# Two decoder blocks on one core: products of zeros ahead of the first unit, another order of the first loads, two query units over six blocks, another start of the banks' turn

## The reference, cut to what matters

```
def first_block(x, ...):                      # shortened
    h = rmsnorm(x, norm_mix_g)
    q, k, v, ... = split_cols(h @ w_in)       # 36 column units of 256
    x = x + merge(moba_attention(q, k, v), hgrn2(...)) @ w_out
    x = x + cross(rmsnorm(x, norm_x_g) @ wq_x, rmsnorm(mem, norm_mem_g) @ wkv_x) @ wo_x
    x = x + ffn(rmsnorm(x, norm_ffn_g))
def second_block(x, ...):
    for layer in range(2):
        x = x + 0.5 * swiglu(rmsnorm_2(x, ffn1_norm[layer]), ...)
        x = x + (nsa_mixer, diff_mixer)[layer](rmsnorm_2(x, mix_norm[layer]), ...)
        x = x + 0.5 * swiglu(rmsnorm_2(x, ffn2_norm[layer]), ...)
```

## Time and profile before

| | |
|---|---|
| median of 3 runs | 1664.88 us |
| lowest and highest | 1663.13, 1666.32 us |
| the profiled execution | 1664.09 us |
| its span, first to last instruction | 1662.3 us |
| mean granted clock of TensorE | 0.996 |
| instructions | 27264 |
| HBM | 281 MB read, 170 GB/s over the span |

### The profile page before, as it was taken

One profiled execution on the slowest core, in us unless ns is written; L12 is line 12 of the kernel. 1 busy time (PEld: TensorE's weight loads), 2 busy tenths in 40 slices (PEclk: granted clock), 3 DMA queues, 4 the chain that ended last, 5 costly groups with the idle time before them and its releaser, 6 DMA issues.

```text
span 1662.3 us, 27264 instructions
## 1 busy us (share of the span) xinstructions
PE 1626.0 (98%) x11542; PEld 1467.7 (88%) x11542; DVE 1222.1 (74%) x1481; ACT 929.5 (56%) x1249; POOL 153.4 (9%) x63
## 2 busy tenths in 40 slices
PE   7999999999999999999999899999999999999999
PEld 7999989999988888888987688888888898788888
DVE  6888868674588768986578868866887667678864
ACT  6966778455544455444387854444544457764442
POOL 0000000000022101220000002210222000002210
PEclk9999999999999999999999899999999999999999
DMA  7454434444355455545542235545554564345544
GB/s 258 180 199 153 153 129 151 178 172 159 129 204 199 140 192 212 208 163 173 199 178 103 103 120 195 192 153 202 209 197 160 177 223 146 109 147 185 192 157 130
DMA packets 44617, 283.80 MB, mean 171 GB/s; under 512 B 4944, under 2 KB 6608, under 8 KB 17744
## 3 DMA queue, kind: packets, MB, share of 16 engines
q1 hardware_dynamic: 44352, 281.99, 47.9%
q10 hardware_dynamic: 144, 0.08, 0.0%
HBM read 281.00 MB, written 1.05 MB: 170 GB/s over the span
## 4 chain that ended last, share of the span: by engine, by line
PE 83%; DVE 8%; ACT 7%; issue 2%; DMA 0%; DVEq 0%; ACTq 0%
PE bank L511 82%; ACT WH L1198 3%; DVE WL L1787 2%; DVE STAT L1945 1%; ACT SB L1323 1%; DVE HT L1843 0%; PE bank L676 0%; ACT XR L1205 0%; ACT XM L1205 0%; DVE XM L1795 0%; DVE SB L1942 0%; ACT FB L1222 0%; DVE FB L1813 0%; DMA PAR<-in_par 0%; DVE FA L2241 0%
## 5 line engine op out<-in xcount | busy, mean ns | idle before, releaser
L1787 DVE TENSOR_TENSOR WL<-RAW,WH 128x2048 fp32r<-128x2048 f32 (+1 forms) x282 | 590.0, 2095 | 165.3 <-ACT WH L1198 161.0
L1198 ACT ACTIVATE WH<-RAW 128x2048 fp32r<-128x2048 f32 (+1 forms) x282 | 494.1, 1755 | 360.6 <-PE bank L511 354.8
L511 PE MATMUL bank<-XR,WH 128*128 128x256 f32 (+1 forms) x2608 | 647.6, 327 | 12.2 <-DVE WL L1987 11.0
L511 PE MATMUL bank<-XR,WL 128*128 128x256 f32 x1832 | 515.6, 281 | 0.0
L511 PEld LDWEIGHTS bank<-XR,WH 128*128 128x128 f32 x2608 | 437.3, 189 | 58.4 <-DVE WL L1987 11.0
L511 PEld LDWEIGHTS bank<-XR,WL 128*128 128x128 f32 x1832 | 346.7, 189 | 0.1
L511 PE MATMUL bank<-XF,WH 128*128 128x512 f32 x880 | 305.3, 392 | 0.0
L511 PE MATMUL bank<-XM,WH 128*128 128x512 f32 (+1 forms) x960 | 290.9, 363 | 2.4 <-DVE XM L1828 1.3
L511 PE MATMUL bank<-XF,WL 128*128 128x256 f32 x880 | 246.0, 280 | 0.0
L511 PE MATMUL bank<-XM,WL 128*128 128x256 f32 x832 | 232.6, 280 | 0.0
L511 PEld LDWEIGHTS bank<-XM,WH 128*128 128x128 f32 x960 | 171.3, 188 | 32.9 <-DVE XM L1795 1.9
(11 more groups left out here) (285 smaller groups left out, 1719.6 us busy)
## 6 DMA issues: line engine op xcount, KB each, us to landing
RAW<-in_f1i SPq DMA_DIRECT2D x44, 1024.0 KB, 4.8
RAW<-in_f2i SPq DMA_DIRECT2D x44, 1024.0 KB, 4.8
RAW<-in_w_in SPq DMA_DIRECT2D x35, 1024.0 KB, 4.8
RAW<-in_w_ffn_in SPq DMA_DIRECT2D x22, 1024.0 KB, 4.8
RAW<-in_f1o SPq DMA_DIRECT2D x32, 704.0 KB, 4.2
RAW<-in_f2o SPq DMA_DIRECT2D x32, 704.0 KB, 4.2
RAW<-in_diff_w_in SPq DMA_DIRECT2D x12, 1024.0 KB, 4.9
RAW<-in_w_ffn_out SPq DMA_DIRECT2D x16, 704.0 KB, 4.2
```

What stands on the lines that cost most here:

```text
L511: return e.matmul(o, l, r, start=start, stop=stop)
L1198: e.activation(split_at(u, cols)[0], RAW[:, u % NRAW, 0:cols], ACT.Copy).then_inc(hi_done.tick(u), 1)
L1787: e.tensor_tensor(lo, RAW[:, u % NRAW, 0:cols], hi.bitcast(f32), sub).then_inc(lo_done.tick(u), 1)
```

## The change

Four edits. (1) `warm()`: DVE clears 128 x 256 of a scratch tile; PE, once ACT has done two pieces of x, multiplies that tile by itself six times into bank 7, which is not read. These are plain f32 products. (2) The constants' load is issued behind unit 1 and not ahead of it. (3) `first_two`: the first two query units of the cross attention run their products on blocks 0 to 5 of x one after the other, then unit 0 those on blocks 6 and 7, the norm's sum, and unit 1 those on blocks 6 and 7. Before, the order was unit 0, the norm's sum, unit 1. (4) In diff the turn of "main" starts at its third bank and that of "pair" at its first.

```
+            def first_two(names, x, x_name, events, between):
+                held = []
+                for k0, k1 in ((0, 6), (6, 8)):
+                    for z, name in enumerate(names):
+                        if k0 == 0:
+                            held.append((*weights(name), take("main", name)))
+                        u, w, b = held[z]
+                        for m, k in sorted(((m, k) for m in range(2) for k in range(k0, k1)), key=lambda mk: in_order_of_x(*mk)):
+                            q.wait_ge(parts, (x_name, k))
+                            t = mm2(b[:, m * 256:m * 256 + 256], at_k(w, k, m * 128, 128), at_k(x, k, 0, 256), k == 0 and m == 0, k == 7 and m == 1)
+                        if k1 == 8:
+                            t.then_inc(used.tick(u), 1)
+                            empties(name, events[z])
+                            if z == 0:
+                                between()
...
+        BLANK = SQ[:, 0:256]
+            def warm():
+                q.wait_ge(blank, 0)
+                q.wait_ge(xhi, ("mix", 1))
+                for n in range(WARM):                      # WARM = 6
+                    t = mm(banks[7][:, 0:256], BLANK[:, 0:128], BLANK[:, 0:256])
+                t.then_inc(warmed.tick(0), 1)
...
+            warm()
             for s, (g, n) in enumerate(ORDER):
...
-            for n in range(4):
-                unit_T(("wq_x", n), two(XS), "x", 8, (rscaled, ("qx", n)), order=in_time if n else in_order_of_x)
-                if n == 0:
-                    norm_sum("x")
-                if n >= 2:
-                    cross_scores(n - 2)
+            first_two([("wq_x", n) for n in range(2)], two(XS), "x", [(rscaled, ("qx", n)) for n in range(2)], lambda: norm_sum("x"))
+            for n in range(2, 4):
+                unit_T(("wq_x", n), two(XS), "x", 8, (rscaled, ("qx", n)))
+                cross_scores(n - 2)
...
-            turn["main"], turn["pair"] = 0, 1
+            turn["main"], turn["pair"] = 2, 0
             diff_unit(0, "main")
...
+            e.memset(BLANK, 0.0).then_inc(blank.tick(0), 1)
             q.wait_ge(small["par"], 0)
...
                 if u == 0:
                     e.dma_start(RAW[:, 0, 0:1024], src[:, 0:1024]).then_inc(small["w0"].tick(0), 16)
                     e.dma_start(RAW[:, 0, 1024:2048], src[:, 1024:2048]).then_inc(raw[0].tick(0), 16)
-                    load("con", CON[:, :], A["con"])
                 else:
                     e.dma_start(RAW[:, u % NRAW, 0:cols], src).then_inc(raw[u % NRAW].tick(u), 16)
+                if u == 1:
+                    load("con", CON[:, :], A["con"])
```

More of the change, by code:

```diff
@@ L130 @@
 NRAW, NW = 3, 3
+WARM = 6
 LAGS = {"moba": 2, "nsa": 5, "diff": 4}
@@ L339, in program @@
         sr_done = signal("sr")
+        blank = signal("blank")
+        warmed = signal("warmed")
         block = ctx.enter_context(nc.Block())
```

## The result

The changed kernel took 1660.83 us in the median of 14 runs (1659.75 to 1663.66), the kernel before 1665.47 (1663.13 to 1666.36, 14 runs) in the same comparison: a ratio of 0.9976, 95% interval 0.9969 to 0.9983. By that ratio it is faster by 4.0 us (2.8 to 5.2); the two medians are 4.6 apart, the means 3.8. The forecast was 1662.9, in a range of 1660.6 to 1665.4; its sum was 1.95 us. The time fell into the range, but the gain is about twice the forecast's, and that has to be explained.

What follows compares the result with a forecast made beforehand. PE, busy 98% of the span, was taken to bound the kernel. Start -2.1, queries -1.5, diff's start +1.65 and diff's end 0 gave -1.95 us, so 1662.9 in medians, range 1660.6 to 1665.4.

Steps and rivals of the forecast that it cites:

- rival 4: Start: products of zeros do not raise the clock; +0.4 there, +0.55 in all, time 1665.4; chance 8%.
- Diff's start: First product of diff waits for DVE to add the ffn's last sum from bank 2: +1.65 us, ends 0 and +1.8.
- Diff's end: ("diff_w_out", 3) starts 1.5 us earlier, but DVE's work holds the next norm's sum: 0, ends 0 and -1.5.
- rival 1: Diff's end pays after all, or its start's wait is soaked up by later PE waits: 1661.4; chance 12%.
- the queries: Cross attention's first query units: unit 1's 12 triples fill unit 0's waits, -1.5 us, ends 0 and -1.5.
- the start: Zeros raise the clock by 12.2, constants load later, so the first unit ends at 17.4, not 19.49: -2.1 us.
- rival 2: Start's gain mostly lost because second or third unit's weights come late: -0.9 in place of -2.1, 1664.1; chance 10%.
- rival 3: Start: the clock rises earlier than 12.2, giving -2.5 in place of -2.1, time 1662.5; chance 15%.

Runs made afterwards that it cites:

- 14 early products: Changed kernel with diff's old bank order and 14 zero products waiting for the memset alone, not for x: mean 1660.34 us, ratio to before 0.9972.
- the banks' kernel: Kernel before with only diff's bank order changed (edit 4 alone): mean 1665.74 us, ratio to before 1.0005.
- the early split: Diff's old bank order, ACT splitting the third unit's weights right behind the norm's squares: 1660.34 us with 14 zeros behind the memset, 1661.67 with zeros behind x.
- the second comparison: Runs on another chip of before (mean 1665.21 us), the changed kernel again, it with diff's old bank order, and both kernels with 14 zero products.

## Why the prediction was right or wrong

**Held.** Zeros raise the clock: rival 4 fell with the first trace, and in both traces with 14 early products the rise came with nothing but zeros run (at 4.7 and 5.7). Diff's start costs 1.67 (forecast 1.65), and nothing of it is hidden later: from diff's first norm's sum to the 2.71 us wait there are 93.72 to 93.82 us with and 93.81 to 93.84 without the banks' turn. Diff's end by itself pays nothing: with no dip in either, the stretch behind that wait takes 31.95 without the turn and 31.90 with it, although the 48 products start 1.6 us earlier. That was the forecast's reason (DVE's work up to the norm's sum), and rival 1 fell with it.

**Off in size: the queries.** 1.9, not 1.5 (between the norm's sums 161.75 to 162.06 us in five traces without the edit, 159.98 in the trace of the edit alone). The whole stretch of XS products went from 26.50 (360.27 to 386.77) to 24.73 (358.43 to 383.16), 1.8 less. The forecast's 1.5 was the gap in unit 0 up to the norm's sum. What it left out is the pause behind that sum (0.35 us to the next product, now 0.24) and a slightly closer spacing (0.357 us a triple, now 0.355); and the profiled trace had one of the two smallest gaps of five: 7.20 us from unit 0's first product to the norm's sum, 7.21 in one other and 7.39 to 7.41 in three.

**Off in size: the start.** -2.1 was forecast, and against the trace that it was read from the changed kernel's second norm's sum is 1.66 earlier. But that run's first unit was the slowest of five traces with this start (norm's sum at 23.81, 24.28, 24.34, 24.79, 25.09, with a first product at 10.9 to 11.1 in each), since the rise of the clock, where the spacing of the products changes, came at 14.2 in the first of them and at 17.15 in the last: a spread of about 2.9 us. Over the five, the second norm's sum stands at 290.46 and not at 291.06; in the four traces with zeros, constants and no other edit of the start it stands at 288.31 to 289.61, 289.16 in the mean: -1.3. The mean times say -1.6 +- 0.7.

So 0.6 of the 0.8 missing from the trace's -2.1 are the base, one late rise taken as the usual one. The other 0.2 are two errors that partly cancel. The rise was put at 12.2 and came at 9.8 to 11.5 in these four, which brought the first unit's norm's sum to 22.67 in the mean, 2.4 before the profiled run's. And 0.5 of that were lost on the way to the second one: in one of the four the third unit's weights were late by 0.50, as rival 2 had it by less ("0.4 us are spare"; in the others they were done only 0.05 to 0.2 ahead), and in two the slower triples took 0.7 more.

The Trainium skill (TensorE: Matmul & The Clock Gate, what is actually happening) says that the point of the rise varies between runs. The traces agree: without zeros it came 3.3 to 6.1 us behind the first product. In the six traces whose zeros wait for x it lay inside the zeros or within the first triple behind them, so rival 3's mechanism held as well. A sum made against one run of such a start carries an error of +-0.6 us from that alone.

**Missing: the dip at 1445.** The stretch of the 2.71 us wait was read for its waits and not for its clock, though the trace had the fall at 1447 to 1451. It costs 1.3 to 1.6 us up to the last norm's sum, and the changed kernel has not had it in two traces of two.

**The sum once more.** Start -1.3 to -1.6, queries -1.9, diff's start +1.67, diff's end 0, dip -1.5: -3.0 to -3.3, and -3.65 +- 0.5 is measured, 1.7 beyond the forecast's -1.95. Most of these 1.7 are the dip, which the forecast priced at nothing; that the start gave 0.5 to 0.8 less and the queries 0.4 more than forecast nearly cancels. That the forecast's time came so near is in part luck: it lacked a term about as large as its own ones. The dip's price is from traces. By the means of the banks' kernel alone the turn gave back 0.9 +- 0.5 (1.67 - 0.8).

**Open.** Why the banks' turn keeps that dip away is not settled. PE's work and waits from diff's first norm's sum to the dip are the same in both to 0.1 us; what differs is that they come 1.67 us later behind the work before. One trace without the turn had no dip either, and the turn's mean, +0.8 +- 0.5, lies above the +0.2 that 1.67 - 1.5 would give, so it is not kept away in each run or not by the turn alone. That it is a matter of when the stretch comes is my reading; no run shifted diff alone by another amount.

**The better kernel.** It is probably the one without the banks' turn. The four kernels with the first three edits and the old turn have a mean of 1660.76 +- 0.4 over 36 runs (19 of these with the early products, 22 with the early split), against 1661.28 +- 0.5 of the changed one: 0.5 +- 0.6. Within the second comparison it is 1660.36 (25 runs) against 1661.45 (11 runs): 1.1 +- 0.7. The turn alone cost 0.8 +- 0.5. So the first three edits are worth the whole gain, and the fourth, its wait and its missing dip taken together, costs some 0.5 to 1.1.

## What to carry to other kernels

A swap of banks that ends a wait pays only if nothing else keeps the work behind it; read what the next common point waits for before counting the wait as a gain, and price the new wait fully if PE has no slack there. Products ahead of the real work should last until it starts: let them wait for something that comes just before it, since in two of three traces with an idle gap behind them the clock fell again, and the start lost most or all of what they had won. Beside the waits, read the granted clock of the stretch: a wait can cost half its own length again in the work behind it (1.3 to 1.6 us behind 2.71 here), in some runs and not in others, so that an edit of 2 us is judged by the traces' distances and many runs, not by one profiled time.

## What the runs showed of the hardware

The granted clock fell behind a short idle time: 1.86 us of it at the start, after 8 us of nearly unbroken products, was enough in one run, and 1.37 us was not in another. With 4.54 us it fell inside them. In the middle of the program it fell in or behind a wait of 2.71 us in ten of fourteen traces, and from 920 on in all fourteen, where the longest single wait from 905 to the fall is 0.85 us in the trace of before but PE stands still again and again. Products of zeros raised the clock as the others do: with 14 of them and nothing else run, it rose at 4.7 and at 5.7, 3.5 and 4.5 us behind the first. Six, begun at 6.5 to 7.0, took 4.2 to 5.5 us where 5.5 is half speed throughout, and the first unit behind them ran at 0.35 us a triple, from its first or second one on. Six that began at 1.2 and ended at 6.7 ran at half speed to their end. The point of the rise differed by 2.9 us between five runs whose first product came at the same time to 0.3 us.
